# End of routing in a one-core decoder layer: block 0's half gate and down product moved, list rows by one load, third gather ahead of the row addition

## The reference, cut to what matters

```
x1     = x + gt1 * mix
h2     = rmsnorm(x1) * (1 + sc2) + sh2
logits = h2 @ w_router + b_router           # 32 experts, top 4, softmax over the four
gu     = h2[tokens of e] @ w_gate_up[e] + b_gate_up[e]
act    = min(glu, 7) * sigmoid(1.702 * glu) * (clip(lin, -7, 7) + 1)
y      = act @ w_down[e] + b_down[e]
out    = rmsnorm(x1 + gt2 * sum of y * weight)
```

## Time and profile before

| | us |
|---|---|
| runs, median (lowest to highest) | 2314.43 (2310.81 to 2315.14) |
| profiled execution, own time | 2316.25 |
| its span, first to last instruction | 2314.4 |
| TensorE busy | 2200.6 (95%) |
| DVE, ACT, GpSimd busy | 1029.5, 333.1, 849.1 |
| mean granted TensorE clock | 0.981 |

### The profile page before, as it was taken

The page is one execution under the profiler, slowest core; times in us unless marked ns, Lnnn a source line. Parts: engine busy times, 40 slices in busy tenths (PEclk is TensorE's granted clock), DMA queues, the critical chain, the costliest instruction groups (busy, mean ns, idle before and its releaser), DMA issues.

```text
span 2314.4 us, 80327 instructions
## 1 busy us (share of the span) xinstructions
PE 2200.6 (95%) x31685; PEld 1502.2 (65%) x31685; DVE 1029.5 (44%) x3487; ACT 333.1 (14%) x919; POOL 849.1 (37%) x1658
## 2 busy tenths in 40 slices
PE   6999989999899899999999999999999999999995
PEld 2777776666544467777777777767675567775573
DVE  2464237777255434343434343434443344443344
ACT  0000017777211000000000000000000000000001
POOL 2011006554224443434343434344443344443433
PEclk9999998999999999999999999999999999999998
DMA  9531051000336787686768686878979978989996
GB/s 312 191 137 58 12 158 35 1 2 1 116 107 229 275 289 250 218 282 224 274 220 287 215 286 213 289 253 276 380 250 355 377 272 317 381 305 390 390 379 224
DMA packets 183488, 534.03 MB, mean 231 GB/s; under 512 B 30152, under 2 KB 59216, under 8 KB 183248
## 3 DMA queue, kind: packets, MB, share of 16 engines
q1 hardware_dynamic: 143472, 479.09, 55.7%
q0 software_dynamic: 33360, 39.96, 8.2%
q10 hardware_dynamic: 6480, 12.72, 1.9%
HBM read 498.27 MB, written 33.34 MB: 230 GB/s over the span
## 4 chain that ended last, share of the span: by engine, by line
PE 55%; DMA 14%; issue 2%; SPq 1%; POOL 1%; DVE 1%; POOLq 0%; another core or an unknown queue 0%; ACT 0%; DVEq 0%; ACTq 0%
PE psum L1701 34%; PE psum L1713 17%; DMA w_ring<-in_w_gate_up 8%; DMA w_ring<-in_w_down 4%; PE psum L1259 4%; DMA x_gathered<-h_rows,scalars_i 1%; SPq L1583 0%; DVE x L1399 0%; POOL slot_list L1214 0%; DMA x<-x_rows 0%; PE psum L1268 0%; DMA token<-k_pairs 0%; SPq L1145 0%; DMA x_rows<-y_out,scalars_i 0%; SPq L1608 0%
## 5 line engine op out<-in xcount | busy, mean ns | idle before, releaser
L1701 PE MATMUL psum<-w_ring,xT 128*32 128x320 f32 (+1 forms) x18304 | 1023.7, 381 | 19.2 <-issue 14.7
L1701 PEld LDWEIGHTS psum<-w_ring,xT 128*32 128x32 f32 x18304 | 696.6, 110 | 340.7 <-issue 41.5
L1713 PE MATMUL psum<-w_ring,actT 128*32 128x256 f32 x9152 | 531.0, 382 | 17.3 <-DMA w_ring<-in_w_down 15.7
L1713 PEld LDWEIGHTS psum<-w_ring,actT 128*32 128x32 f32 x9152 | 349.8, 111 | 152.6 <-DMA w_ring<-in_w_down 20.7
L1642 POOL TENSOR_TENSOR scalars<-scalars 128x1 f32<-128x1 f32 x575 | 108.9, 189 | 728.8 <-DVE xT L1768 562.6
L1754 DVE TENSOR_TENSOR glu<-psum,expert_bias 128x160 f32<-128x160 f32 (+1 forms) x286 | 83.1, 291 | 537.8 <-PE psum L1701 537.7
L1748 ACT ACTIVATE glu<-glu 128x160 f32<-128x160 f32 (+1 forms) x286 | 88.7, 310 | 1444.3 <-DVE glu L1756 1429.7
L1659 POOL DMA_INDIRECT x_rows<-y_out,scalars_i x142 | 228.0, 1606 | 47.2 <-issue 46.9
L783 POOL TENSOR_SCALAR scores<-scores,coef 128x64 f32<-128x64 f32 (+5 forms) x128 | 134.1, 1063 | 137.5 <-DVE coef L992 137.5
L1650 POOL DMA_INDIRECT x_gathered<-h_rows,scalars_i x144 | 153.3, 1064 | 81.3 <-issue 79.2
L1776 DVE TENSOR_TENSOR psum<-psum,expert_bias 128x256 f32<-128x256 f32 x143 | 61.8, 432 | 242.2 <-PE psum L1713 223.4
(11 more groups left out here) (246 smaller groups left out, 1882.7 us busy)
## 6 DMA issues: line engine op xcount, KB each, us to landing
w_ring<-in_w_gate_up SPq DMA_DIRECT2D x128, 1280.0 KB
w_ring<-in_w_down SPq DMA_DIRECT2D x128, 1024.0 KB
w_ring<-in_w_gate_up SPq DMA_DIRECT2D x128, 768.0 KB
ada_then_cmp_in<-in_w_ada SPq DMA_DIRECT2D x16, 1024.0 KB, 6.3
expert_bias<-bias_by_quarter ACTq DMA_DIRECT2D x128, 96.0 KB
ada<-in_w_ada SPq DMA_DIRECT2D x8, 1024.0 KB, 5.6
xt<-in_x SPq DMA_DIRECT2D x8, 512.0 KB, 6.3
w_uv_then_w_out<-in_w_in SPq DMA_DIRECT2D x4, 1024.0 KB, 9.5
```

Source lines behind the costliest of these rows:

```text
L1701: last = nc.tensor.matmul(psU[h][j * BLK:(j + 1) * BLK, :], xT[:, k, :], w[:, j], start=(k == 0), stop=(k == KD - 1))
L1713: last = nc.tensor.matmul(psO[m * BLK:(m + 1) * BLK, :], actT[h][:, i, :], w[:, m * Q:(m + 1) * Q], start=(k == 0), stop=(k == KD - 1))
```

## The change

Four edits, all at the seam:

1. DVE makes block 0's half 0 gate right behind the tile loop, ahead of `assign` of tile 6, and ACT its Gelu ahead of the copies of tile 7. TensorE multiplies half 0 of block 0's down product ahead of the counts by place, and half 1 behind them.
2. The value load for expert 0's list stands between the last two scatters.
3. List rows come by one DMA to 128 partitions, whose source is repeated four times, in place of four DMAs; also for the first rows and in the loop.
4. The gather of block 2 stands ahead of the row addition of block 0, and so does `take_rows`.

```diff
@@ block.gpsimd @@
         tiles(pool, body)
         scatter(TILES - 2, 0)
+        lines = parts.lines_of(pool, 0)
         scatter(TILES - 1, 1)
         for i in range(2):
             pool.wait_ge(s_sc[i], 16 * TOPK * TILES // 2)
             pool.wait_ge(s_xnst[i], 16 * TILES // 2)
-        parts.load_rows(pool, 0)
+        parts.load_lines(pool, 0, lines)
         pool.wait_ge(s_spare, 48)
         for i in range(2):
             pool.wait_ge(s_x1st[i], 16 * TILES // 2)
-        parts.add_rows(pool, 0, 7)
         parts.take_rows(pool, 0)
         pool.wait_ge(parts.s_ids, 4)
-        parts.gather(pool, 2, 10)
+        parts.gather(pool, 2, 7)
+        parts.add_rows(pool, 0, 10)
         parts.load_rows(pool, 1)
@@ block.tensor @@
         nc.tensor.matmul(psR[0:E, E:E + 2], total_b[0][:], ones[:, 0:2], start=True, stop=True).then_inc(s_cnt, 1)
+        pe.wait_ge(parts.s_actT[0], 1)
+        parts.down(pe, 0, 0)
         pe.wait_ge(s_halves, 1)
...
         last.then_inc(s_cnt, 1)
-        parts.down_both(pe, 0, 0)
+        pe.wait_ge(parts.s_actT[1], 1)
+        parts.down(pe, 0, 1)
@@ block.scalar @@
         tiles(act, body)
+        parts.activation(act, 0, 0)
         copy_h2(TILES - 1, 1)
         copy_logits(TILES - 1)
         weights(TILES - 1, 1)
-        for b in range(FIRST):
-            parts.activations(act, b)
+        parts.activation(act, 0, 1)
+        parts.activations(act, 1)
@@ block.vector @@
         tiles(dve, body)
+        dve.wait_ge(parts.s_bias[0], 64)
+        parts.gates(dve, 0, 0, 0)
         assign(TILES - 2, 0)
...
-        dve.wait_ge(parts.s_bias[0], 64)
-        parts.gates(dve, 0, 0, 0)
         parts.gates(dve, 0, 1, 0)
@@ expert_parts @@
+    def load_lines(pool, e, lines):
+        pool.dma_start(rows_f[e % 2][:].rearrange("p b c -> p (b c)"), lines.partition_broadcast(4)).then_inc(s_rows, 16)
+
     def load_rows(pool, e):
-        lines = lines_of(pool, e)
-        for q in range(4):
-            pool.dma_start(rows_f[e % 2][q * BLK:(q + 1) * BLK, :, :].rearrange("p b c -> p (b c)"), lines
-                           ).then_inc(s_rows, 16)
+        load_lines(pool, e, lines_of(pool, e))
 
     def load_first_rows(pool):
         lines = lines_of(pool, 0)
-        for q in range(4):
-            pool.dma_start(rows_f[0][q * BLK:(q + 1) * BLK, 0:FIRST, :].rearrange("p b c -> p (b c)"), lines[:, 0:2 * FIRST]
-                           ).then_inc(s_rows, 16)
+        pool.dma_start(rows_f[0][:, 0:FIRST, :].rearrange("p b c -> p (b c)"), lines[:, 0:2 * FIRST].partition_broadcast(4)
+                       ).then_inc(s_rows, 16)
...
+    def activation(act, b, h):
+        act.wait_ge(s_glu[h], b + 1)
+        n = ACT_TILES[h] * BLK
+        nc.scalar.activation(glu[:, 0:n], glu[:, 0:n], ACT.Gelu_apprx_sigmoid).then_inc(s_gate[h], 1)
+
     def activations(act, b):
         for h in range(2):
-            act.wait_ge(s_glu[h], b + 1)
-            n = ACT_TILES[h] * BLK
-            nc.scalar.activation(glu[:, 0:n], glu[:, 0:n], ACT.Gelu_apprx_sigmoid).then_inc(s_gate[h], 1)
+            activation(act, b, h)
```

More of the change, by code:

```diff
@@ L1662, in take_first_rows @@
     def take_first_rows(pool):
-        pool.wait_ge(s_rows, 64)
+        pool.wait_ge(s_rows, 16)
         nc.gpsimd.tensor_tensor(rows_f[0][:, 0:FIRST, 0], rows_f[0][:, 0:FIRST, 0], quarter[:, 0:1].to_broadcast([P, FIRST]), ALU.add
@@ L1679, in take_rows @@
         if part != 1:
-            pool.wait_ge(s_rows, 64 * (e + 2))
+            pool.wait_ge(s_rows, 16 * (e + 2))
             nc.gpsimd.tensor_tensor(rows_f[e % 2][:, :, 0], rows_f[e % 2][:, :, 0], quarter[:, 0:1].to_broadcast([P, EDGES]), ALU.add
@@ L1786, in expert_parts @@
         gather, add_rows, take_first_rows, take_rows, load_next, up, down_both)
+    parts.lines_of, parts.load_lines, parts.activation, parts.down, parts.s_actT = lines_of, load_lines, activation, down, s_actT
     parts.load_bias, parts.load_gate, parts.activations, parts.gates, parts.transpose_x, parts.weigh, parts.quarter, parts.s_c = (
```

## The result

Over 22 executions of each, the changed kernel takes 2317.27 us (2312.24 to 2322.67) where the kernel before takes 2313.47 (2310.81 to 2318.23). The ratio is 1.0015 [1.0008, 1.0022]: 3.5 us slower, where 3 us faster was forecast. The difference lies within the 0.2% that the forecast called no change, but the time lies outside its range (2308.5 to 2315). The profiled execution took 2319.45 with a span of 2317.5; mean granted clock 0.980.

The account below looks back on a forecast made before the run. The prediction took block 3's start, set by the chain of waits between 753 and 790 us, to decide the end: 790.08 - 787.0 = 3.1 us gained, 3 us off the median 2314.43, so 2311.4 us; range 2308.5 to 2315.

Parts of the forecast that it names:

- What bounds the kernel: Behind 790 us one train of TensorE work and weight streams; whatever block 3's start gains or loses at 790.08 reaches the end.
- Scatter to list rows: Between last scatter's landing and first list load: value load hidden in GpSimd's idle time, 0.6 us saved; list landed at 769.2.
- list rows to block 2: Row addition no longer ahead of index arithmetic: gather 2 issues at 771.5 instead of 774.73, rows ready 3.2 us earlier.
- The wait of 3.17 us before the last placing: Wait before placing the last tile, releaser unnamed in the profile; if it changes, the forecast end would be wrong.
- TensorE up to block 2: Earlier half gate and split down product end block 0 at 763.3, not 767.4; block 2 starts at 775.4 against 778.66.
- ACT: Gelu between two Exps takes two more table loads, 1.28 us each, covered by idle time and the wait: costs nothing.
- Block 3: Addition ahead of expert 1's list load, landing 2.5 us; gather 3 issues at 780.0, block 3 starts 787.0 instead of 790.08.
- rival B: Row addition behind gather 2 takes back its gain: list landing 4 us, 1 us gained, 2313.4; chance 0.15.
- The sum: Block 3's start gains 3.1 us, between 2.5 and 4.1, carried to the end: 0.13%, 2311.4 us.
- C: Single list load lands later, its 128 rows moved by fewer DMA engines; gain falls by 0.8 to 2.3: 2312.1; chance 0.14.
- D: TensorE's own end decides block 3 (4.1), and a released stream or clock dip falls better: 5 us, 2309.4; chance 0.16.
- E: TensorE's clock stays at 1.2 GHz past 775.2, gain gone; up to 784.4 it costs 4.6 us: 2319; chance 0.07.

Follow-up runs that it names:

- the three faster kernels: Changed kernel with single list loads only for first rows and experts 0 and 1: row addition behind expert 1's list load, 0.9990; old addition order, 0.9981 and again 0.9988.
- the four idle waits: Kernel before with four already met waits on each of GpSimd, TensorE, ACT and DVE ahead of the experts: 2311.85 us, 0.9991.

## Why the prediction was wrong

**What bounds the kernel:** right. Delays at the seam reached the end, and so did gains where the closing stretch stayed short: TensorE's block 3 started 1.7 to 2.6 us earlier in the three faster kernels, and they took 2.3 to 4.4 us less.

**Scatter to list rows; list rows to block 2:** right, with some luck in the starting point. List load at 767.22 (forecast 767.4), landed 769.6 (769.2), gather 2 at 771.64 (771.5). The wait of 3.17 us before the last placing, on which the forecast said that everything hangs, had shrunk in this execution (the idle time there was 3.26 us before):

```profile
754.68 0.29 DVE L1438 TENSOR_TENSOR prod<-hot,psum 128x128 f32<-128x128 f32 x1 [0.83 <-PE psum L1294]
```

The last scatter was issued 2.4 us earlier for it, at 760.90, but the store of h2 rows landed at 766.44 and took its place. The wait doesn't go with the change: it is 3.70 us in the second profile of the changed kernel and 0.05 with the four idle waits. Its cause is open. Hiding the value load took the 1.43 us to 0.8, as worked out; it does so in every kernel with edit 2.

**TensorE up to block 2:** partly. The half gate used its cover up: gate from 747.10 to 749.11, assign of tile 6 at 749.04 with no idle time, and alone it made no difference. Block 0's down product was to have its weights; in this execution it waited for them four times, so block 1 started 2.3 us late, and block 2 at 777.12 instead of 775.4. It cost nothing, since block 3's rows came later still (0.67 us of idle time).

**ACT:** right. Three table loads of 1.28 us, and Exp at 751.85 ahead of the last placing. The Trainium skill, ScalarE: Activation LUTs, What ACT_TABLE_LOAD costs, adds a drain of 1.38 us to each; here the rows around them are

```profile
745.28 0.19 ACT L1372 ACTIVATION_READ_ACCUMULATOR wexp<-below_top 128x1 f32 x1
745.48 1.28 ACT L1751 ACT_TABLE_LOAD   x1
```

with 0.01 us between, so this trace shows no drain.

**Block 3:** this step failed. "Landing took 2.72 there; 1.8 is the lower bound; I take 2.5, since the addition's own traffic is ahead." The list load behind the addition took 4.15 us to land in the first profile; from its issue to the quarter's addition it was 4.3, 5.5 and 5.0 us in the three profiles with this order and single loads, against 2.8 with the addition behind it. The rest of the step was right to 0.4 us: addition to 775.2 (775.1), list load issued inside it at 774.71 (775.1), gather 3 to block 3 7.06 us (7.0). This is rival B, which had 4 us for the landing and still expected 1 us gained. Over the three profiles with this order and a single load, block 3 stands at 21.4, 23.6 and 23.9 in the table, mean 22.9, where the kernel before has 23.0 and 22.8, and 23.0 with the four idle waits: everything that gather 2 won (2.6 to 2.9 us) was lost by gather 3. In two of the three TensorE idled for 4 us and lost another 1.7 us in block 3, 8.80 for 7.11; the granted clock was 0.83 over the stretch from 788 to 798 of one of them.

The kind of mistake is plain in the kernel before: there the addition's issue filled the time in which the list rows were landing, so it was nearly free (0.8 us at gather 2). Ahead of the list load it fills no wait. The forecast charged its issue there, and for the later landing 0.7 us (2.5 for 1.8), where the runs show 1.5 to 2.7 (4.3 to 5.5 for 2.8).

**The sum:** a term was missing. "Carried to the end" is true of the seam, but the end moved: the closing stretch is 1.87 us longer in every kernel with single loads throughout, and the forecast has nothing for it. With no gain at the seam that gives 1.9 us slower; 3.5 and 4.6 were measured. The 8.80 for 7.11 us in two of three profiles adds 1.1 us in the mean. The other 0.5 to 1.6 us are within the intervals, and open. So is this: from one profile and one ratio for each kernel, the measured time lies between 3 us below and 4 us above what PE 3 and the closing stretch give. It lies above in most, by 2.3 us for the half gate alone and 1.3 for the order alone; of the kernels with nothing moved it is 3 us below for the four idle waits and equal for the other.

**Rivals C, D, E:** C fell with the single load alone, 2.5 us ahead at the seam; the first list load of the changed kernel landed in 2.38 us, under the 2.5 that would have spoken for C. How many DMA engines carried it, no run here shows. D and E didn't show: block 1's up product took 8.28 us, 1.2 more than at full clock, where 1.5 was forecast, and the granted clock was 1.00 over 768 to 776.

## What to carry to other kernels

When an operation is moved off one leg of a chain, look at what its issue was hiding behind: an issue that lies inside another transfer's landing time is nearly free (0.8 us here), and the same issue in front of the next transfer is paid twice, once as queue time and once as a later landing. Put the load whose answer you wait for first, and fill its wait with the work that nobody waits for: block 3's rows come earliest when the addition stands behind the list load. Then look at whether the consumer can use it: here TensorE couldn't start much earlier, and the times don't tell that order from the old one. And compare the last stretch of two traces, from the last transfer to the end, before looking for a loss in between; take a second profile of the unchanged kernel before explaining a difference of 2 us.

## What the runs showed of the hardware

The closing stretch behind GpSimd's last transfer isn't a constant: 4.62, 4.64, 5.40, 6.48 and 6.60 us for 464, 455, 400, 365 and 496 transfers issued by GpSimd, each repeatable to 0.02 us where more than one kernel had the same count (eight with 464, six with 365, four with 455). What sets it is open.

A list load to 128 partitions, 256 bytes each, took 2.5 to 2.9 us from issue to use when no addition was ahead of it in GpSimd's queue since the scatter, 2.6 to 4.3 us when one was two transfers ahead (old order, five profiles), and 4.3 to 5.5 us when one was directly ahead (three profiles).
